# Group norms in the z stage of a Mamba-2 / DeltaNet block: four sums with places of their own, one root for all, and the late panels dealt out anew

## The reference, cut to what matters

```python
(z_s, xbc, dt_s, qkv, z_d, b_d, a_d, gate_s, gate_d) = jnp.split(u @ w_in[l], split_points, axis=-1)
...
# mamba2_branch: y is the scan's output, 2048 wide; four groups of 512
yg = (y.reshape(b, S, SSM_INNER) * jax.nn.silu(z.astype(f32))).reshape(b, S, SSM_GROUPS, -1)
yg = yg * lax.rsqrt(jnp.mean(yg * yg, axis=-1, keepdims=True) + EPS)
return (yg.reshape(b, S, SSM_INNER) * norm_w.astype(f32)).astype(z.dtype)
...
# deltanet_branch: q, k of 8 heads of 128 are normalised, then used in chunks
q = l2_norm(q.reshape(b, S, DN_HEADS, DN_HEAD_K)) * (DN_HEAD_K ** -0.5)
k = l2_norm(k.reshape(b, S, DN_HEADS, DN_HEAD_K))
...
M = jnp.where(strict, jnp.einsum("bnhid,bnhjd->bnhij", kb, k) * decay, 0.0)
sol = lax.linalg.triangular_solve(eye + M, rhs, left_side=True, lower=True, unit_diagonal=True)
a_qk = jnp.einsum("bnhid,bnhjd->bnhij", q, k) * decay
```

## Time and profile before

| | us |
|---|---|
| median of 3 runs | 2302.59 |
| lowest, highest | 2299.76, 2304.95 |
| the profiled execution | 2300.63 |
| its span | 2298.70 |
| TensorE busy | 2154.1 |
| DVE busy | 1341.4 |
| ACT busy | 1159.0 |

### The profile page before, as it was taken

One profiled execution on the slowest core, in us unless ns is written; L12 is line 12 of the kernel. 1 busy time (PEld: TensorE's weight loads), 2 busy tenths in 40 slices (PEclk: granted clock), 3 DMA queues, 4 the chain that ended last, 5 costly groups with the idle time before them and its releaser, 6 DMA issues. The chain is left out here.

```text
span 2298.7 us, 41083 instructions
## 1 busy us (share of the span) xinstructions
PE 2154.1 (94%) x15684; PEld 1885.5 (82%) x15684; DVE 1341.4 (58%) x1853; ACT 1159.0 (50%) x1703; POOL 61.3 (3%) x74
## 2 busy tenths in 40 slices
PE   6999889999999998988999999999999987999998
PEld 4787778878888977878998887887997886998887
DVE  3436465555557966564655555555886566556555
ACT  3454544445445566653545445445557663535444
POOL 0000000000000010000000000000011000000000
PEclk9999999999999998998999999999999998999999
DMA  9653245545553544321455554554454322254553
GB/s 401 244 229 108 83 148 189 193 165 187 193 186 130 182 145 140 119 75 57 149 183 192 193 188 167 190 192 148 165 183 129 137 86 74 74 184 183 186 193 124
DMA packets 53328, 373.24 MB, mean 162 GB/s; under 512 B 6304, under 2 KB 6304, under 8 KB 9280
## 3 DMA queue, kind: packets, MB, share of 16 engines
q1 hardware_dynamic: 47664, 342.00, 41.2%
q0 software_dynamic: 5520, 29.23, 3.6%
HBM read 370.10 MB, written 1.11 MB: 161 GB/s over the span
## 5 line engine op out<-in xcount | busy, mean ns | idle before, releaser
L1411 ACT ACTIVATE HI<-ring 128x1024 fp32r<-128x1024 f32 x614 | 633.0, 1054 | 782.1 <-PE banks L535 399.4
L1955 DVE TENSOR_TENSOR LO<-ring,HI 128x1024 fp32r<-128x1024 f32 x326 | 398.8, 1225 | 374.1 <-ACT HI L1411 368.5
L1961 DVE TENSOR_TENSOR LO<-ring,HI 128x2048 fp32r<-128x2048 f32 x139 | 318.5, 2291 | 272.8 <-ACT HI L1411 272.7
L499 PE MATMUL banks<-UH,HI 128*128 128x256 f32 x1456 | 428.0, 294 | 1.8 <-issue 1.8
L500 PE MATMUL banks<-UL,HI 128*128 128x256 f32 x1456 | 417.0, 286 | 0.0
L501 PE MATMUL banks<-UH,LO 128*128 128x256 f32 x1456 | 416.4, 286 | 0.0
L533 PE MATMUL banks<-HI,UH 128*128 128x512 f32 x896 | 350.0, 391 | 7.1 <-DVE LO L1961 4.9
L535 PE MATMUL banks<-HI,UL 128*128 128x512 f32 x896 | 349.4, 390 | 0.0
L534 PE MATMUL banks<-LO,UH 128*128 128x512 f32 x896 | 349.4, 390 | 0.0
L499 PEld LDWEIGHTS banks<-UH,HI 128*128 128x128 f32 x1456 | 284.7, 196 | 20.6 <-issue 19.8
L500 PEld LDWEIGHTS banks<-UL,HI 128*128 128x128 f32 x1456 | 284.9, 196 | 1.2 <-issue 1.2
(11 more groups left out here) (325 smaller groups left out, 3065.5 us busy)
## 6 DMA issues: line engine op xcount, KB each, us to landing
ring<-in_w_stream SPq DMA_DIRECT2D x315, 1024.0 KB, 4.8
ARENA<-in_ada_stream POOLq DMA_DIRECT2D x16, 1024.0 KB, 5.1
ARENA<-in_ada_stream SPq DMA_DIRECT2D x8, 1024.0 KB, 15.2
GRMS<-cum_rows POOLq DMA_DIRECT2D x16, 256.0 KB, 3.6
ARENA<-in_na_bias POOLq DMA_DIRECT2D x2, 1024.0 KB, 14.9
RMS<-cum_rows POOLq DMA_DIRECT2D x8, 256.0 KB, 3.4
RSTD<-cum_rows POOLq DMA_DIRECT2D x8, 256.0 KB, 3.6
ARENA<-in_ropes POOLq DMA_DIRECT2D x1, 1088.0 KB, 20.4
```

Source lines behind the costliest of these rows:

```text
L499: nc.tensor.matmul(out, lh, rh, start=start, stop=False, **kw)
L1411: nc.scalar.activation(HI[:, q % PARTS, at], ring[:, q % RING, at], ACT.Copy).then_inc(hi_ready, 1)
L1955: nc.vector.tensor_tensor(LO[:, q % PARTS, at], ring[:, q % RING, at], HI[:, q % PARTS, at].bitcast(F32), ALU.subtract).then_inc(lo_ready, 1)
L1961: nc.vector.tensor_tensor(LO[:, q % PARTS, :], ring[:, q % RING, :], HI[:, q % PARTS, :].bitcast(F32), ALU.subtract).then_inc(lo_ready, 2)
```

## The change

- The four group sums get places of their own: the halves (256 columns) of banks 6 and 7, `GROUP_AT`. The head sums use the left halves of these banks before. So sums 1 to 3 wait for a query/key root instead of a group root (sums are counted 0 to 3 in the code and 1 to 4 in the prediction's words "third sum", "fourth sum"). Spreads move to banks 0 to 3.
- One ACT instruction takes all four roots at the end, 128x1024 over banks 6 and 7, and raises `yrms_ready` by four. The roots land in `GRMS` in another order (`GROUP_SLOT`), which the group norm follows.
- Within a turn TensorE does the spread first, then the group sum, then the head sums.
- The fourth group sum moves from behind the z stage to behind the first half of late panel 0 and head products 0. The second half of late panel 0 stands between it and head products 1, and that now carries the wait for the root. Late panels 1 and 2 are dealt out differently between head products 2 and 3 and the turns.
- In the last turn ACT takes the SiLU first, and splits late panel 1 in two halves around the squares of group 3. DVE splits that panel behind its last query/key norm.

```diff
-GROUP_BANKS = (0, 0, 7, 0)
-Q_BANKS = (1, 2, 3, 6)
+GROUP_AT = ((7, 1), (6, 1), (6, 0), (7, 0))
+GROUP_SLOT = (3, 1, 0, 2)
+Q_BANKS = (0, 1, 2, 3)
...
                 def group_sum(g):
-                    if g == 2:
-                        pe.wait_ge(qkrms_ready, 2 * l + 2)
-                    elif g:
-                        pe.wait_ge(yrms_ready, 4 * l + (g + 1) // 2)
+                    if g:
+                        pe.wait_ge(qkrms_ready, 2 * l + (2 if g == 3 else 1))
                     pe.wait_ge(ysq_ready, 4 * l + g + 1)
+                    b, column = GROUP_AT[g]
...
                 for j in range(L_ZS):
                     wide(w0 + L_CONV + j, Q_LAYERS + LQ_WIDE + L_CONV + j, rounds, j % 2)
+                    if 4 <= j:
+                        qk_spread(j - 4)
+                    if j % 2 == 1 and j >= 3:
+                        group_sum((j - 3) // 2)
                     if 1 <= j <= 4:
                         mm = head_sums2(j - 1)
                         if j % 2 == 0:
                             mm.then_inc(qkss_done, 1)
-                    if j % 2 == 1 and j >= 3:
-                        group_sum((j - 3) // 2)
-                    if 4 <= j:
-                        qk_spread(j - 4)
-                group_sum(3)
-
-
-                pe.wait_ge(yrms_ready, 4 * l + 4)
-                pe.wait_ge(qk_ready, 4 * l + 4)
...
                 def head_products(g):
 
-                    if g >= 2:
+                    if g == 0:
+                        pe.wait_ge(qk_ready, 4 * l + 4)
+                    elif g == 1:
+                        pe.wait_ge(yrms_ready, 4 * l + 4)
+                    else:
...
+                late_wide(0, 0)
                 head_products(0)
+                group_sum(3)
+                late_wide(0, 1)
                 head_products(1)
-                late_panel(0)
                 values_turn(0)
                 values_turn(1)
-                late_wide(1, 0)
+                late_panel(1)
                 head_products(2)
-                late_wide(1, 1)
+                late_wide(2, 0)
                 head_products(3)
-                late_panel(2)
+                late_wide(2, 1)
                 values_turn(2)
...
-                def group_rms(g):
-                    act.wait_ge(yss_done, 4 * l + g + 1)
-                    nc.scalar.activation(GRMS[:, g, :], bank[GROUP_BANKS[g]][:, 0:S], ACT.Sqrt,
-                                         bias=EPST[:, :]).then_inc(yrms_ready, 1)
+                def group_rms():
+                    act.wait_ge(yss_done, 4 * l + 4)
+                    nc.scalar.activation(GRMS[:, :, :].rearrange("p (b g) n -> p b (g n)", b=2), bank_pair[3][:, :, :], ACT.Sqrt,
+                                         bias=EPST[:, :]).then_inc(yrms_ready, 4)
...
                 for j in range(L_ZS):
-                    ahead(LQ_WIDE + L_CONV + j)
+                    if j < L_ZS - 1:
+                        ahead(LQ_WIDE + L_CONV + j)
...
-                    if j in (4, 6):
-                        group_rms((j - 4) // 2)
+                split_half(Q_LAYERS + LQ_WIDE + L_CONV + L_ZS - 1 + PARTS, 0, rounds)
                 group_squares(3)
-                group_rms(2)
-                group_rms(3)
+                split_half(Q_LAYERS + LQ_WIDE + L_CONV + L_ZS - 1 + PARTS, 1, rounds)
+                group_rms()
...
                 for j in range(L_ZS):
-                    ahead(LQ_WIDE + L_CONV + j)
+                    if j < L_ZS - 1:
+                        ahead(LQ_WIDE + L_CONV + j)
...
+                ahead(LQ_WIDE + L_CONV + L_ZS - 1)
```

More of the change, by code:

```diff
@@ L1082, in group_sum @@
                 def group_sum(g):
-                    if g == 2:
-                        pe.wait_ge(qkrms_ready, 2 * l + 2)
-                    elif g:
-                        pe.wait_ge(yrms_ready, 4 * l + (g + 1) // 2)
+                    if g:
+                        pe.wait_ge(qkrms_ready, 2 * l + (2 if g == 3 else 1))
                     pe.wait_ge(ysq_ready, 4 * l + g + 1)
+                    b, column = GROUP_AT[g]
                     for e in range(4):
                         at = g % 2 * 1024 + e * S
-                        mm = nc.tensor.matmul(bank[GROUP_BANKS[g]][:, 0:S], MEAN_G[:, :], SQ[:, at:at + S], start=(e == 0),
+                        mm = nc.tensor.matmul(bank[b][:, column * S:column * S + S], MEAN_G[:, :], SQ[:, at:at + S], start=(e == 0),
                                               stop=(e == 3))
@@ L2444, in group_norm @@
                     dve.wait_ge(yrms_ready, 4 * l + g + 1)
-                    need(step(nc.vector.reciprocal(GRMS[:, g, :], GRMS[:, g, :])))
+                    rms = GRMS[:, GROUP_SLOT[g], :]
+                    need(step(nc.vector.reciprocal(rms, rms)))
                     for e2 in range(4):
                         x_ = CONV[:, 4 * g + e2, :]
-                        ins = nc.vector.scalar_tensor_tensor(x_, x_, pk2("ssm_norm", 4 * g + e2), GRMS[:, g, :],
+                        ins = nc.vector.scalar_tensor_tensor(x_, x_, pk2("ssm_norm", 4 * g + e2), rms,
                                                              ALU.mult, ALU.mult)
```

## The result

| | before | changed |
|---|---|---|
| median, us | 2302.59 | 2286.95 |
| lowest, highest | 2299.76, 2304.95 | 2286.46, 2291.31 |
| runs | 5 | 5 |
| span of the profiled execution | 2298.7 | 2284.8 |
| ratio, 95% interval | | 0.9941 (0.9927 to 0.9954) |

The changed kernel is 0.6% faster: 15.6 us by the medians, 13.9 us by the spans, 10.6 to 16.8 us by the interval. The forecast was 13.0 us, 2289.6 with a range of 2285.5 to 2295.5. The sign and the range held, and the forecast was 2.7 us too high. (The five runs of the kernel before have the same median, lowest and highest as the three named ahead of the prediction.)

What follows compares the result with a forecast made beforehand. TensorE, 94% busy, bounds the kernel; only its waits and low clock can be won back. Gains of 7.40 to 7.7 us per layer, less 1.16 and 0.1, were taken as 6.5, 13.0 for two layers: 2289.6 us, range 2285.5 to 2295.5.

Steps and rivals of the forecast that it cites:

- The wait for the squares and the low clock: At the fourth group sum: 3.9 us of waiting, and 2.18 us of low clock and root wait, go per layer.
- The wait before head products 2: TensorE's wait for the first turned values goes, as a whole panel now lies between: 0.7 us per layer.
- The wait before spread 2: In turn 6, the wait for query/key norm 1 goes, since a SiLU table load goes: 0.62 us per layer.
- The root, hidden: ACT's one root and its load, 2.4 to 2.5 us after sum 4, hidden before head products 1, 0.4 to spare.
- The new wait: Values turn 1 waits for DVE's segment step 1: 1.16 us lost per layer, bounds 1.0 to 1.3.
- Spreads 2 and 3: Spreads now precede group sums and may wait for query/key norms: 0.1 us together per layer, bounds 0 and 0.6.
- Values turn 3: It would come about 0.3 us after the second decayed row, so without a wait.
- no drain: Rival, chance 0.07: 1.4 us more at the root's table load makes head products 1 wait 1.0 per layer, 2291.6 us.
- no wait at the norms: Rival, chance 0.06: TensorE waits 0.5 us more at each of spreads 1 to 3, 1.5 per layer, 2292.6 us.
- none at values turn 3: Rival, chance 0.06: ACT and DVE hold TensorE up at values turn 3 by 1 to 2 us, 2291.6 to 2293.6.
- the start of the inverse: Rival, chance 0.04: the inverse's start hangs on something else and eats the gain, within 0.2% of 2302.6 us.
- a low clock brought by the new wait: Rival, chance 0.03: the clock stays low over late panels 1 to 3, 7.5 us slower per layer, 2317.6 us.

Runs made afterwards that it cites:

- e1: Kernel before, with only the first half of late panel 0 moved ahead of the fourth group sum: median 2293.10 us against 2301.41 for the kernel before.
- e8: Changed kernel with ACT's and DVE's last turn as before, whole split of late panel 1 first: median 2291.08 us, stage 86.17 us per layer.
- e4: Changed kernel with TensorE's order behind the z stage as before, late panel 0 whole after head products 1: median 2288.08 us, stage 85.42 us.
- e2: Changed kernel with dummy one-column roots in turns 4 and 6, bringing the table loads back: median 2286.60 us, stage 85.64 us.
- e3: Changed kernel with the second half of late panel 0 behind head products 1, so nothing covers the root: median 2294.49 us, stage 86.76 us.
- e6: Changed kernel with the group sum ahead of the spread again in turns 5 and 7: median 2287.70 us, stage 84.95 us.
- e5: Changed kernel with sum 4, then head products 0 and 1, between the halves of late panel 0: median 2285.94 us, stage 84.06 us.
- e7: Changed kernel with the root uncovered, plus a dummy root ahead of the wait for sum 4: median 2289.89 us, stage 85.45 us.

## Why the prediction was right

- **The wait for the squares and the low clock** (3.90 + 2.18). Right, and e1 shows that they are one thing: without the idleness, no low clock. Sum 4 is now 1.54 us before a panel product, where I had reckoned 1.82 from sum 3, which stands before a spread, so the second term measures 4.00 - 1.54 = 2.46. The reason given for the wait was incomplete: it named ACT's split and table load. The rows of DVE show that DVE's split of late panel 1 held the product of the SiLU, and e8 that the load was hidden behind it. The change moves DVE's split too, so this did not touch the sum.
- **The wait before head products 2** (0.7). Gone. e4 brings it back as 0.74, with half a panel in front instead of a whole one.
- **The wait before spread 2** (0.62, through one SiLU load). Right, with its mechanism: e2 puts the loads back and gets 0.63 us. Counted from start to start it was 0.91 - 0.21 = 0.70 us, since 0.21 is the normal step from a product to a spread, and not 0.12 as I had it.
- **The root, hidden.** Right: 1.12 us for the 1.1 I had, behind a load of 1.28. e3 measures 2.54 us without cover, for 2.4 to 2.5. The margin was 0.2 us, not 0.4. The reader came 1.54 + 3.06 = 4.60 us after sum 4 began, where I had 1.82 + 2.91 = 4.73, and the root was done after 4.39 us, where I had 4.2 to 4.3.
- **The new wait** at values turn 1. The right place, and a bit too dear: 1.16 us expected, 0.94 measured. DVE started 0.20 us after head products 1, and TensorE 0.06 after DVE, where I had put 0.28 and 0.15.
- **Spreads 2 and 3**: 0.1 us expected, none measured. Both norms were ready some 0.2 us ahead. e6 shows that the order within a turn has no price.
- **Values turn 3**, called 0.3 us away from a wait: the decayed row ended at 990.53, the turn started at 990.87, no wait. Even 0.9 us earlier (e5) nothing waits, because that whole chain hangs on head products and moves along.

The net was forecast as 6.5 us per layer and came out at 6.9 and 7.0. The new wait was 0.22 us smaller, the spreads cost 0.1 less, and the term of sum 4 was 0.28 larger. Against that the two halves of late panel 0 took 3.06 us each and not 2.91, 0.30 together. The rest, some 0.2, is in the steps from one kind of product to the next. Both layers lie above the bounds of 5.5 to 6.7, and the median lies 2.3 us under the 2289.2 that they give. It is inside the range because the range was widened for the scatter of the runs. The forecast of the time was 2.7 us over the median measured: 1.0 of that is the net of the stages, and 1.7 is what the medians show beyond the stages (15.6 against 14.0), which stays open.

The rivals: no drain (e3, e7), no wait at the norms, none at values turn 3, and the start of the inverse moved along with the gain (84.95 us, and 84.06 in e5). The one that ended slower, a low clock brought by the new wait, did not come. The clock was full over 0.78 us of idleness in the changed kernel and over 2.54 in e3.

## What to carry to other kernels

A wait for a small result at the end of a stage is cheapest filled with half of the next big piece that needs nothing from it. Look also at what the low clock adds: here 3.1 us less of waiting were worth 4.4 (e1). When a result goes back and forth between engines (SiLU on ACT, product on DVE, squares on ACT, sum on TensorE), put the steps of that chain first in the last turn of each of them, and the split of the panel that nobody wants yet behind them. To find what held a step, read the rows of every engine on the chain: here the wait list named ACT, and DVE's own split had set the time. One of the two measures was nearly enough, so ask before adding the second what it still covers.

Before ordering ACT's work by its functions, look for the load whose reader waits: four went per layer, and putting them back cost time at one. And measure between two instructions that stand in every variant: a stage told 0.1 us, where the medians of five runs could not tell 2.

## What the runs showed of the hardware

- A table load on ACT took 1.28 us and nothing came with it, also when it stood behind a wait (2.54 against 1.26 us at its reader).
- A root of 128x1024 from two neighbouring PSUM banks takes 1.12 us, four of 128x256 took 0.47 each.
- 2.54 us of idleness left the granted clock at 1.00; 3.90 us brought slices of 0.86 and 0.72, and the sum behind them took 3.43 us instead of 1.89.
- Outside the stage one and the same kernel varied by 4.7 us between two of its profiles, in the 800 us from the first stage to the second.
